# mLSTM row sums in a two-layer hybrid trunk: VectorE adds the overlapping blocks of the weights, TensorE multiplies their sum by ones

## The chip, the cores and the metric

The kernel runs on one core of a Trainium2 chip. The metric is the device time of one launch in microseconds (us), lower is better. Engines are named as in the profile: PE is TensorE (PEld its weight loads), DVE is VectorE, ACT is ScalarE, POOL is GpSimd, SP is SyncE, which here only starts loads of weights.

## The reference, cut to what matters

The program is a decoder trunk of two layers over 512 tokens and a width of 2048. Each layer projects the normalised input to 7944 columns, runs four groups of mixers on them (latent attention, RWKV-7, mLSTM, differential attention), gates them, and projects back. The change is in the mLSTM group, which has four heads of width 128. The reference works it in chunks of 64 tokens with a carried state. What it computes of one head is this:

```python
D = b[..., :, None] - b[..., None, :] + ig[..., None, :]
D = jnp.where(mask, D, -jnp.inf)
...
s = jnp.einsum('bhcjd,bhcsd->bhcjs', q, k) * jnp.exp(D - m_j[..., None])
num = jnp.einsum('bhcjs,bhcsv->bhcjv', s, v) + ...   # state carried from earlier chunks
den = jnp.sum(s, axis=-1) + ...
h = num / jnp.maximum(jnp.abs(den), jnp.exp(-m_j))[..., None]
```

`den` is the sum of the weights of each query token over all key tokens up to it. The kernel leaves the chunks away and forms the whole causal 512 x 512 matrix of weights of a head at once, with key tokens on the partitions, and then needs its sum over the keys, once for every query token, spread over all 128 partitions.

## The kernel before, in words

TensorE has one long job, and small ones are slipped into it. The long job is the projections: 640 steps of weights in two layers (one step is 128 rows of the contraction and up to 512 columns of weights), each with 4 tiles (one group has 3) of three 512-column matmuls (weights and activations are split in a high and a low half, `w_hi`, `w_lo`, `h_hi`, `h_lo`; L769, and L784 for the output projection). SyncE loads each step into `raw`. GpSimd makes both halves of it (L728 the high one, L738 the low one, which subtracts the high half from `raw`); there are four buffers of halves, so GpSimd runs at most four steps ahead of TensorE. ScalarE copies a finished group of projections out of PSUM (L1218) and stores it.

The small jobs are the mixers. Between two of their steps TensorE runs a number of projection tiles that is written down in a table (`FILL`), by `fill(name, head)`; these tiles are what it does while VectorE and ScalarE work on the mixer. Every engine runs its instructions in the written order and waits on semaphores; `link` makes VectorE wait for its own last instruction.

One head of the mLSTM goes like this, with its lines:

- L1120 and L1121: two matmuls spread the gates over the partitions. VectorE takes a running maximum (L1913, L1914), forms four blocks of exponents in `ml_w` (L1917) and finishes q and k (L1923). TensorE runs `fill("ml_qk")` meanwhile. ScalarE exponentiates `ml_w` (L1537, L1539).
- L1127: four matmuls give the scores. Key block i (128 keys on the partitions) meets only queries from i * 128 on, so the blocks are 512, 384, 256 and 128 columns wide. VectorE multiplies them by `ml_w` into `ml_s` (L1927) and masks the diagonal block (L1928), and the last of these raises `s_ml_s_ready`. TensorE runs `fill("ml_s")` meanwhile, 8, 7, 7 or 6 tiles.
- L1135: four matmuls, 1280 columns together, add values times weights into PSUM bank 0. L1138: four matmuls of the same widths multiply the weights by a matrix of ones into bank 1, which is the sum over the keys; the last raises `s_ml_num_mm`. All of them are plain fp32, which the trace shows as two matmul instructions each.
- VectorE meanwhile runs the convolution of the next head's q and k, eight instructions (L1901 and L1903), except in the last head. Then it waits for `s_ml_num_mm`, forms the denominator (L1936, L1937), its reciprocal (L1938), `ml_h` (L1939) and its square (L1940). TensorE runs `fill("ml_h")` meanwhile, 14, 13, 12 or 11 tiles.
- L1145: one matmul by ones sums the squares. ScalarE makes the norm's factor (L1263, L1264), then runs what the table gives it (`fill("ml_gate")`), and VectorE gates the head (L1943, L1944, L1624 to L1636). Then the next head begins with L1120, which waits for the gate's L1631.

In the first head the fill's last tiles finish a group of projections: ScalarE copies three of its four tiles out before the norm's factor and the fourth behind it, and TensorE's next group waits for these copies.

Of the kernel before, what the change touches and what calls it, by code (L numbers as in the profile page):

```python
# [27 lines left out]
P = 128  # L28
D, T, DEPTH = 2048, 512, 2
NT = T // P  # L30
# [287 lines left out]
def build(nc, a, out):  # L318

    with ExitStack() as ctx:  # L320
# [50 lines left out]
        ps = ctx.enter_context(nc.psum_tensor("ps", [P, 4, 512], F32))  # L371
# [6 lines left out]
        ident, ones, bones = const("ident"), const("ones"), const("bones")  # L378
# [119 lines left out]
        ml_ucol = rg(NT, 4)  # L498
        ml_m, ml_nf = rg(T), rg(T)
        ml_w = rg(NT, T)  # L500
        ml_s = rg(NT, T)
        ml_h, ml_den, ml_sq = rg(T), rg(T), rg(T)
        ml_o, ml_oe, ml_rs = rg(T), rg(T), rg(T)
# [129 lines left out]
        s_ml_s_ready = sem("ml_s_ready")  # L633
        s_ml_num_mm = sem("ml_num_mm")
# [42 lines left out]
        for layer in range(DEPTH + 1):  # L677
# [9 lines left out]
            with nc.Block() as block:  # L687
# [54 lines left out]
                def _(pe):  # L742
                    mm, turn = nc.tensor.matmul, nc.tensor.transpose
# [87 lines left out]
                    for k in range(4):  # L831
                        for i in range(NT):
                            if not tail and k == 0:
                                pe.wait_ge(s_x_loaded[i], 16)
                            last = turn(ps[:, k, i * P:(i + 1) * P], x_tok[:, i, k * P:(k + 1) * P], ident)
                        last.then_inc(s_x_turned, 1)
                    for n, tiles in enumerate(ROWS_OF_MEAN):
                        pe.wait_ge(s_rs_diag, n + 1)
                        mm(ps_proj[:, n, tiles.start * P:tiles.stop * P], ones, rs_diag[:, tiles, :],
                           start=True, stop=True).then_inc(s_rs_mm, 1)  # L840
                    pe.wait_ge(s_rs_ready, 2)
                    for k in range(4, KT):
                        pe.wait_ge(s_h_scaled, k - 3)
                        for i in range(NT):
                            last = turn(ps[:, k % 4, i * P:(i + 1) * P], x_tok[:, i, k * P:(k + 1) * P], ident)
# [12 lines left out]
                    for half in (slice(0, 64), slice(64, P)):  # L858
                        last = mm(ps[half, 2, :], rot_mla[half, :], la_peg[half, :], start=True, stop=True)
# [7 lines left out]
                    for i in range(NT):  # L867
                        for j in range(2):
                            last = mm(ps[:, i, :], la_in[:, 3 + j, i * P:(i + 1) * P],
                                      la_wkv[:, j, :].rearrange("p (h c) -> p h c", h=HEADS)[:, :, P:2 * P],  # L870
                                      start=(j == 0), stop=(j == 1))
# [17 lines left out]
                    for h in range(HEADS):  # L889
# [8 lines left out]
                        for j in range(2):  # L898
                            last = mm(ps[:, 2, :], la_wkv[:, j, h * 256:h * 256 + P], la_in[:, 3 + j, :],
                                      start=(j == 0), stop=(j == 1))  # L900
# [40 lines left out]
                    for hp in range(4):  # L941
# [53 lines left out]
                        for i in range(NT):  # L995
                            for q, o in swapped:
                                last = mm(ps[o, 3, i * 64:(i + 1) * 64], ident[q, q], rw_xt[q, 4 + i, :],
                                          start=True, stop=True)
# [118 lines left out]
                    for h in range(HEADS):  # L1117
                        if h:
                            pe.wait_ge(s_y_ready, 8 + h)
                        mm(ps[:, 0, :], sel_u[0:36, h * P:(h + 1) * P], ml_gt[0:36, :], start=True, stop=True)  # L1120
                        mm(ps[:, 1, :], sel_f[64:100, h * P:(h + 1) * P], ml_gt[64:100, :], start=True, stop=True  # L1121
                           ).then_inc(s_ml_u_mm, 1)
                        fill("ml_qk", h)
                        pe.wait_ge(s_ml_max, h + 1)
                        pe.wait_ge(s_ml_qk_ready, h + 1)
                        for i in range(NT):
                            last = mm(ps[:, i, i * P:T], ml_acc[:, 1, i * P:(i + 1) * P], ml_acc[:, 0, i * P:T],  # L1127
                                      start=True, stop=True)
                        last.then_inc(s_ml_scores_mm, 1)
                        fill("ml_s", h)  # L1130
                        pe.wait_ge(s_ml_s_ready, h + 1)
                        if h == 0:
                            pe.wait_ge(s_ml_first_loaded, 16)
                        for i in range(NT):
                            mm(ps[:, 0, i * P:T], ml_v[:, i, h * P:(h + 1) * P], ml_s[:, i, i * P:T],  # L1135
                               start=(i == 0), stop=(i == NT - 1))
                        for i in range(NT):
                            last = mm(ps[:, 1, i * P:T], ones, ml_s[:, i, i * P:T],  # L1138
                                      start=(i == 0), stop=(i == NT - 1))
                        last.then_inc(s_ml_num_mm, 1)  # L1140
                        if h == 0:
                            fill("to_z_ml")
                        fill("ml_h", h)
                        pe.wait_ge(s_ml_h_sq, h + 1)
                        mm(ps[:, 2, :], ones, ml_sq, start=True, stop=True).then_inc(s_ml_h_sum, 1)  # L1145
                        fill("ml_gate", h)
# [462 lines left out]
                def _(dve):  # L1609
# [3 lines left out]
                    def link(ins):  # L1613

                        counts[0] += 1
                        ins.then_inc(s_dve_order, 1)
                        dve.wait_ge(s_dve_order, counts[0])
# [292 lines left out]
                    for h in range(HEADS):  # L1910
# [15 lines left out]
                        for i in range(NT):  # L1926
                            link(v.scalar_tensor_tensor(out=ml_s[:, i, i * P:T], in0=ps[:, i, i * P:T], scalar=0.25 * float(P) ** -0.5, in1=ml_w[:, i, i * P:T], op0=MUL, op1=MUL))  # L1927
                            ins = v.tensor_tensor(ml_s[:, i, i * P:(i + 1) * P], ml_s[:, i, i * P:(i + 1) * P], causal, MUL)  # L1928
                            if i == NT - 1:
                                ins.then_inc(s_ml_s_ready, 1)  # L1930
                            else:
                                link(ins)
                        if h < HEADS - 1:
                            convolve(h + 1)
                        dve.wait_ge(s_ml_num_mm, h + 1)
# [91 lines left out]
```

## Time and profile before

| what | value |
|---|---|
| median of 3 runs | 2431.85 us (2427.43 to 2432.50) |
| the profiled execution | 2427.41 us, its span 2425.6 us |
| PE busy | 2351.5 us, 97% of the span |
| POOL, DVE, ACT busy | 1732.2, 1158.1, 634.4 us (71%, 48%, 26%) |
| mean granted clock of TensorE | 0.993 |
| DMA | 117 GB/s on average |

The profiled execution is at the lower end of the three timed ones. TensorE is the engine that is busy nearly all the time. The page's slices of TensorE's clock are all 9, that is 90% or more of full speed; the short spells at half speed are seen only in narrower windows. A line of the timeline says when a group of like instructions began, how long it took from the first begin to the last end, and in square brackets how long the engine had been idle before it and what released it. Matmuls overlap, so the pace is read from one begin to the next.

### The profile page before, as it was taken

The numbers are of one execution on the slowest core, as the hardware profiler recorded it, in microseconds if no ns is written. First come the engines' busy times: TensorE is split into PE (matmuls) and PEld (weight loads), VectorE is DVE, ScalarE is ACT, GpSimd is POOL, SyncE is SP. The second block draws the span as 40 slices with busy tenths as digits, with TensorE's granted clock in tenths as the row PEclk, the third lists the DMA queues.
The fourth block names the chain that finished last, engine by engine and source line by source line (L and its number), as shares of the span: only waits on it lengthen the run. The fifth ranks groups of instructions, "written<-read, shape, count | busy, mean of one in ns | idle before, by whom it ended". The sixth has DMA issues, their size and how long they took to land. (4 is left out here: it accounts for less than half of the span.)

```text
span 2425.6 us, 38853 instructions
## 1 busy us (share of the span) xinstructions
PE 2351.5 (97%) x16320; PEld 1770.0 (73%) x16320; DVE 1158.1 (48%) x1505; ACT 634.4 (26%) x1124; POOL 1732.2 (71%) x1228
## 2 busy tenths in 40 slices
PE   7999999999999999999999999999999999999999
PEld 5767677777777677777777677777777777777777
DVE  5123345557463675454250232466475547745442
ACT  4222222121221222333241223222122212324321
POOL 3676688668587778777637666877596787888774
PEclk9999999999999999999999999999999999999999
DMA  4623243233233435632445232533232243474223
GB/s 153 189 78 100 79 152 117 75 89 104 81 105 119 127 111 192 218 86 68 140 110 166 79 109 88 157 97 97 67 113 84 84 142 112 133 252 140 79 73 123
DMA packets 163568, 284.18 MB, mean 117 GB/s; under 512 B 28408, under 2 KB 35960, under 8 KB 161856
## 3 DMA queue, kind: packets, MB, share of 16 engines
q1 hardware_dynamic: 108352, 180.93, 26.6%
q10 hardware_dynamic: 55040, 100.77, 12.1%
q8 instruction: 128, 2.10, 0.4%
q14 instruction: 48, 0.39, 0.0%
HBM read 229.97 MB, written 51.64 MB: 116 GB/s over the span
## 5 line engine op out<-in xcount | busy, mean ns | idle before, releaser
L728 POOL TENSOR_SCALAR w_hi<-raw 128x512 fp32r<-128x512 f32 x552 | 903.7, 1637 | 490.8 <-PE ps_proj L769 404.7
L738 POOL TENSOR_TENSOR w_lo<-raw,w_hi 128x512 fp32r<-128x512 f32 (+1 forms) x640 | 832.8, 1302 | 155.0 <-ACT w_hi L1228 99.5
L769 PE MATMUL ps_proj<-h_hi,w_hi 128*128 128x512 f32 (+1 forms) x1760 | 734.8, 418 | 8.0 <-ACT stage L1218 5.0
L769 PE MATMUL ps_proj<-h_lo,w_hi 128*128 128x512 f32 (+1 forms) x1760 | 690.0, 392 | 0.0
L769 PE MATMUL ps_proj<-h_hi,w_lo 128*128 128x512 f32 x1728 | 676.9, 392 | 0.0
L769 PEld LDWEIGHTS ps_proj<-h_hi,w_hi 128*128 128x128 f32 (+1 forms) x1760 | 330.3, 188 | 112.4 <-issue 26.3
L769 PEld LDWEIGHTS ps_proj<-h_lo,w_hi 128*128 128x128 f32 (+1 forms) x1760 | 330.2, 188 | 74.1
L769 PEld LDWEIGHTS ps_proj<-h_hi,w_lo 128*128 128x128 f32 x1728 | 326.3, 189 | 68.7 <-issue 11.1
L784 PE MATMUL ps_proj<-w_hi,h_hi 128*128 128x512 f32 x448 | 184.6, 412 | 9.6 <-DVE arena L1644 9.2
L784 PE MATMUL ps_proj<-w_hi,h_lo 128*128 128x512 f32 x448 | 176.3, 393 | 0.0
L784 PE MATMUL ps_proj<-w_lo,h_hi 128*128 128x512 f32 x448 | 175.8, 392 | 0.0
L784 PEld LDWEIGHTS ps_proj<-w_hi,h_hi 128*128 128x128 f32 x448 | 85.0, 190 | 31.5 <-issue 14.1
L1218 ACT ACTIVATE stage<-ps_proj 128x512 f32<-128x512 f32 (+1 forms) x118 | 70.5, 597 | 136.2 <-PE ps_proj L769 113.8
L769 PE MATMUL ps_proj<-w_hi,h_hi 128*128 128x512 f32 x256 | 104.9, 410 | 0.0
L769 PE MATMUL ps_proj<-w_lo,h_hi 128*128 128x512 f32 x256 | 99.8, 390 | 0.0
L769 PE MATMUL ps_proj<-w_hi,h_lo 128*128 128x512 f32 x256 | 99.8, 390 | 0.0
L784 PEld LDWEIGHTS ps_proj<-w_lo,h_hi 128*128 128x128 f32 x448 | 85.0, 190 | 19.7 <-issue 3.4
L784 PEld LDWEIGHTS ps_proj<-w_hi,h_lo 128*128 128x128 f32 x448 | 84.8, 189 | 18.3
L1717 DVE TENSOR_REDUCE arena<-ps 128x1 f32<-128x128 f32 (+3 forms) x96 | 47.1, 490 | 85.6 <-PE ps L921 60.6
L1228 ACT ACTIVATE w_hi<-raw 128x512 fp32r<-128x512 f32 (+1 forms) x88 | 48.7, 561 | 148.1 <-PE ps_proj L769 75.5
L1263 ACT ACTIVATE arena<-ps 128x512 f32<-128x512 f32 x24 | 14.4, 598 | 242.7 <-PE ps L1102 129.0
L1591 ACT ACTIVATE arena<-ps,arena 128x128 f32<-128x128 f32 (+3 forms) x64 | 38.7, 615 | 129.5 <-DVE arena L1718 129.5
(347 smaller groups left out, 3160.0 us busy)
## 6 DMA issues: line engine op xcount, KB each, us to landing
raw<-in_w_in_dram SPq DMA_DIRECT2D x480, 256.0 KB, 2.7
raw<-in_w_out_dram SPq DMA_DIRECT2D x128, 256.0 KB, 3.0
projected<-stage ACTq DMA_DIRECT2D x116, 256.0 KB, 2.8
arena<-projected ACTq DMA_DIRECT2D x90, 256.0 KB, 3.1
out_dram<-arena ACTq DMA_DIRECT2D x7, 1024.0 KB, 4.8
gated_hi<-arena ACTq DMA_DIRECT2D x24, 256.0 KB, 2.7
gated_lo<-arena ACTq DMA_DIRECT2D x24, 256.0 KB, 3.2
h_hi<-gated_hi SPq DMA_DIRECT2D x8, 768.0 KB, 12.9
```

Of the source, the lines that this page charges most:

```text
L728: nc.gpsimd.tensor_scalar(hi, src, 1.0, None, ALU.mult).then_inc(s_hi_split, 1)
L738: nc.gpsimd.tensor_tensor(lo, src, hi.bitcast(F32), ALU.subtract).then_inc(s_raw_split, 1)
L769: last = mm(ps_proj[rows, m, :], lhsT, rhs, start=(k == 0 and j == 0), stop=(k == KT - 1 and j == len(products) - 1))
L784: last = mm(bank[:, i, :], lhsT, rhs, start=(first and j == 0), stop=(last_k and j == 2))
L1218: nc.scalar.activation(stage[0:rows, m, :], ps_proj[0:rows, m, :], ACT.Copy).then_inc(s_proj_copied, 1)
L1228: nc.scalar.activation(w_hi[:, at_all % N_SPLIT, 0:width], raw[:, at_all % N_RAW, 0:width], ACT.Copy).then_inc(s_hi_by_act, 1)
L1263: link(nc.scalar.activation(dst, src, ACT.Ln, scale=1.0 / n, bias=eps))
L1591: nc.scalar.activation(da_p[:, b, 0:(i + 1) * P], ps[:, b, 0:(i + 1) * P], ACT.Exp, scale=da_rq[:, 4 * half + b:4 * half + b + 1], bias=da ...
L1717: link(v.tensor_reduce(mx[:, b:b + 1], ps[:, b, 0:(i + 1) * P], AX, MAX))
```

## The change

VectorE adds the four blocks of `ml_s` where they overlap. For queries 0 to 127 only block 0 has weights; for queries from 128 on the first addition takes blocks 0 and 1 (384 columns), the second adds block 2 (256), the third block 3 (128). The sum lies in row 0 of `ml_w`, which is free by then. TensorE multiplies 128 columns of block 0 and 384 columns of the sum by ones, in place of 1280 columns. The semaphore `s_ml_s_ready` is raised twice in a head, after the masked weights and after the sum. Everything else, the table of fills too, stays as it is.

```diff
         ml_w = rg(NT, T)
+        ml_sum = ml_w[:, 0, :]
...
                         fill("ml_s", h)
-                        pe.wait_ge(s_ml_s_ready, h + 1)
+                        pe.wait_ge(s_ml_s_ready, 2 * h + 1)
...
-                        for i in range(NT):
-                            last = mm(ps[:, 1, i * P:T], ones, ml_s[:, i, i * P:T],
-                                      start=(i == 0), stop=(i == NT - 1))
-                        last.then_inc(s_ml_num_mm, 1)
+                        mm(ps[:, 1, 0:P], ones, ml_s[:, 0, 0:P], start=True, stop=True)
+                        pe.wait_ge(s_ml_s_ready, 2 * h + 2)
+                        mm(ps[:, 1, P:T], ones, ml_sum[:, P:T], start=True, stop=True).then_inc(s_ml_num_mm, 1)
...
+                        dve.wait_ge(s_ml_s_ready, 2 * h + 1)
+                        link(v.tensor_tensor(ml_sum[:, P:T], ml_s[:, 0, P:T], ml_s[:, 1, P:T], ADD))
+                        link(v.tensor_tensor(ml_sum[:, 2 * P:T], ml_sum[:, 2 * P:T], ml_s[:, 2, 2 * P:T], ADD))
+                        v.tensor_tensor(ml_sum[:, 3 * P:T], ml_sum[:, 3 * P:T], ml_s[:, 3, 3 * P:T], ADD).then_inc(s_ml_s_ready, 1)
                         if h < HEADS - 1:
                             convolve(h + 1)
```

TensorE's instructions around the first head's products, before (L769 is a projection tile, `ps<-arena` the values, `ps<-arena,always` the ones):

```order
L769 MATMUL ps_proj<-h_lo,w_hi 128x512
L1135 MATMUL ps<-arena 128x512 [waits ml_first_loaded,ml_s_ready]
L1135 MATMUL ps<-arena 128x384
L1135 MATMUL ps<-arena 128x256
L1135 MATMUL ps<-arena 128x128
L1138 MATMUL ps<-arena,always 128x512
L1138 MATMUL ps<-arena,always 128x384
L1138 MATMUL ps<-arena,always 128x256
L1138 MATMUL ps<-arena,always 128x128
L769 MATMUL ps_proj<-h_hi,w_hi 128x512
```

And with the change, where all lines of this part are one further down:

```order
L770 MATMUL ps_proj<-h_lo,w_hi 128x512
L1136 MATMUL ps<-arena 128x512 [waits ml_first_loaded,ml_s_ready]
L1136 MATMUL ps<-arena 128x384
L1136 MATMUL ps<-arena 128x256
L1136 MATMUL ps<-arena 128x128
L1138 MATMUL ps<-arena,always 128x128
L1140 MATMUL ps<-arena,always 128x384 [waits ml_s_ready]
L770 MATMUL ps_proj<-h_hi,w_hi 128x512
```

Four matmuls by ones have become two, and the second of them has a wait of its own.

VectorE's instructions in the same place, from the last weights to the denominator, before (L1901 and L1903 are the next head's convolution, L1936 reads the products):

```order
L1927 SCALAR_TENSOR_TENSOR arena<-ps,arena 128x128 [waits dve_order]
L1928 TENSOR_TENSOR arena<-arena 128x128 [waits dve_order]
L1901 TENSOR_SCALAR arena<-arena,par 128x512 [waits ml_qk_loaded]
L1903 SCALAR_TENSOR_TENSOR arena<-arena,par 128x512 [waits dve_order] x3
L1901 TENSOR_SCALAR arena<-arena,par 128x512 [waits dve_order]
L1903 SCALAR_TENSOR_TENSOR arena<-arena,par 128x512 [waits dve_order] x3
L1936 SCALAR_TENSOR_TENSOR arena<-ps,arena 128x512 [waits ml_num_mm]
```

And with the change (L1934 to L1936 are the additions, L1940 is what was L1936):

```order
L1927 SCALAR_TENSOR_TENSOR arena<-ps,arena 128x128 [waits dve_order]
L1928 TENSOR_TENSOR arena<-arena 128x128 [waits dve_order]
L1934 TENSOR_TENSOR arena<-arena 128x384 [waits ml_s_ready]
L1935 TENSOR_TENSOR arena<-arena 128x256 [waits dve_order]
L1936 TENSOR_TENSOR arena<-arena 128x128 [waits dve_order]
L1901 TENSOR_SCALAR arena<-arena,par 128x512 [waits ml_qk_loaded]
L1903 SCALAR_TENSOR_TENSOR arena<-arena,par 128x512 [waits dve_order] x3
L1901 TENSOR_SCALAR arena<-arena,par 128x512 [waits dve_order]
L1903 SCALAR_TENSOR_TENSOR arena<-arena,par 128x512 [waits dve_order] x3
L1940 SCALAR_TENSOR_TENSOR arena<-ps,arena 128x512 [waits ml_num_mm]
```

The three additions stand ahead of the convolution, and so ahead of all that VectorE does for the denominator and the squares.

## Rows read from the trace of the kernel before

**Rows 1.** The page's first part: busy time, share and count.
```profile
PE 2351.5 (97%) x16320; PEld 1770.0 (73%) x16320; DVE 1158.1 (48%) x1505; ACT 634.4 (26%) x1124; POOL 1732.2 (71%) x1228
```

**Rows 2.** TensorE's waits: for whom, us in total, times, longest.
```profile
PE ps L1127 <- DVE arena L1923: 6.4, 4, 2.8
...
PE ps L1145 <- DVE arena L1940: 1.2, 4, 0.3
```

**Rows 3.** Timeline, TensorE, first head: start, duration, count, idle before.
```profile
808.46 2.32 PE L1135 MATMUL ps<-arena 128*128 128x512 f32 x8
810.61 2.32 PE L1138 MATMUL ps<-arena,always 128*128 128x512 f32 x8
...
822.36 1.02 PE L1145 MATMUL ps<-arena,always 128*128 128x512 f32 x2
```

**Rows 4.** Timeline, VectorE, first head.
```profile
806.50 0.29 DVE L1928 TENSOR_TENSOR arena<-arena 128x128 f32<-128x128 f32 x1
...
814.44 0.68 DVE L1936 SCALAR_TENSOR_TENSOR arena<-ps,arena 128x512 f32<-128x512 f32 x1
...
820.00 1.44 DVE L1940 TENSOR_TENSOR arena<-arena 128x512 f32<-128x512 f32 x1
```

**Rows 5.** Timeline, ScalarE, first head.
```profile
823.30 0.60 ACT L1218 ACTIVATE stage<-ps_proj 128x512 f32<-128x512 f32 x1 [0.46 <-ACT stage L1218]
...
825.58 0.60 ACT L1263 ACTIVATE arena<-ps 128x512 f32<-128x512 f32 x1
...
828.03 0.58 ACT L1218 ACTIVATE stage<-ps_proj 128x512 f32<-128x512 f32 x1
```

**Rows 6.** VectorE's groups by shape: busy us, mean ns, idle before.
```profile
L1927 DVE SCALAR_TENSOR_TENSOR arena<-ps,arena 128x384 f32<-128x384 f32 x8 | 4.5, 558 | 0.3
L1927 DVE SCALAR_TENSOR_TENSOR arena<-ps,arena 128x256 f32<-128x256 f32 x8 | 3.4, 425 | 0.3
```

**Rows 7.** Timeline, second head, around the matmul of the squares.
```profile
862.74 1.29 POOL L738 TENSOR_TENSOR w_lo<-raw,w_hi 128x512 fp32r<-128x512 f32 x1
863.12 1.46 DVE L1940 TENSOR_TENSOR arena<-arena 128x512 f32<-128x512 f32 x1
...
864.63 1.12 PE L1145 MATMUL ps<-arena,always 128*128 128x512 f32 x2 [0.34 <-DVE arena L1940]
```

**Rows 8.** Timeline, third head.
```profile
890.11 1.62 DVE L1901 TENSOR_SCALAR arena<-arena,par 128x512 f32<-128x512 f32 x1
890.18 1.26 POOL L738 TENSOR_TENSOR w_lo<-raw,w_hi 128x512 fp32r<-128x512 f32 x1
...
896.38 2.02 POOL L728 TENSOR_SCALAR w_hi<-raw 128x512 fp32r<-128x512 f32 x1 [4.93 <-PE ps_proj L769]
...
903.27 1.13 PE L1145 MATMUL ps<-arena,always 128*128 128x512 f32 x2 [0.25 <-DVE arena L1940]
```

**Rows 9.** Timeline, VectorE, fourth head.
```profile
931.33 0.69 DVE L1936 SCALAR_TENSOR_TENSOR arena<-ps,arena 128x512 f32<-128x512 f32 x1 [4.68 <-PE ps L1138]
```

**Rows 10.** Timeline, TensorE: idle spells and what follows them.
```profile
371.04 0.66 PE L945 MATMUL ps<-arena 32*128 32x512 f32 x1 [3.19 <-ACT arena L1432]
...
828.66 0.50 PE L769 MATMUL ps_proj<-h_hi,w_hi 128*128 128x512 f32 x1 [2.52 <-ACT stage L1218]
...
835.95 0.69 PE L1120 MATMUL ps<-arena 36*128 36x512 f32 x1
...
2029.20 0.50 PE L769 MATMUL ps_proj<-h_hi,w_hi 128*128 128x512 f32 x1 [2.52 <-ACT stage L1218]
...
2034.89 0.69 PE L1120 MATMUL ps<-arena 36*128 36x512 f32 x1
...
2377.73 0.47 PE L784 MATMUL ps<-w_hi,h_hi 128*128 128x512 f32 x1 [2.18 <-PEq L2002]
```

**Rows 11.** Windows of 2 us: busy PE, PEld, DVE, ACT, POOL; PEclk, DMA, GB/s.
```profile
830.00:832.00 2.00, 2.00 (x6) 1.52 (x6) 1.93 (x3) 0.00 (x0) 1.92 (x2) 0.50 0.08 31
...
2030.00:2032.00 2.00, 2.00 (x10) 1.65 (x9) 1.92 (x3) 0.00 (x0) 1.67 (x1) 1.00 0.35 131
```

## The prediction

> **What bounds the kernel now.** The page's first part comes first: TensorE is busy for 2351.5 us of a span of 2425.6, 97%, and VectorE for about half of it [rows 1]. So an instruction taken from TensorE is a gain unless TensorE then waits for somebody else, and the next view is the list of its waits. Two of its lines lie in the mLSTM: TensorE waits for VectorE four times, 1.2 us in all, ahead of L1145, the sum of the squares, and at L1127 [rows 2]. L1145 stands right behind the place of the change, and what it waits for is VectorE's chain, which the change makes longer. So the third view is the timeline of each head, TensorE beside VectorE, to find how much room is left at L1145. Both layers show the same four heads within 0.1 us, apart from spells of slow clock, so I work out one layer and double it.
>
> **What TensorE saves.** L1135 begins at 808.46 and L1138 at 810.61: 2.15 us for 1280 columns of fp32 [rows 3]. The matmuls by ones fall from 1280 to 512 columns, so 768/1280 x 2.15 = 1.29 us a head go, 10.3 us over eight heads.
>
> **What VectorE gets.** Three additions of 384, 256 and 128 columns. The nearest rows are L1927 with two inputs and the same widths, 558 and 425 ns [rows 6], and L1928, which is just such an addition of two blocks in SBUF: 0.29 us for 128 columns [rows 4]. With some 0.04 us between linked instructions: 0.56 + 0.43 + 0.29 + 0.12 = 1.40 us a head. That is the low end. The high end is from L1940: 1.44 and 1.46 us in the first two heads [rows 4, 7], where L1936 with as many columns takes 0.68 [rows 4]. It overlaps a subtraction of GpSimd's: it runs from 862.74 to 864.03 and L1940, begun at 863.12, ends at 864.58, half a microsecond behind it [rows 7]. L1901 at 890.11 takes 1.62 us and ends 0.3 us behind the subtraction of 890.18 to 891.44 [rows 8]. Less 0.56 us or so for its own work, that is a hold of about 1.1 us, and the one of L1940 is 0.8. One such meeting more or less is the unknown in each head: 1.4 us, or 2.5.
>
> The Trainium skill, on the page "SBUF — State Buffer", section "Who interferes with whom", gives the rule behind this: a VectorE instruction with two SBUF inputs contends with a GpSimd instruction that reads SBUF, and the later one waits for the whole of the earlier. The rows above agree in the length of the hold. All three additions are of that kind, and the multiplications with a PSUM input, whose durations stand in for them in the low sum, are not; by the rule alone the low end is too low whenever a subtraction is under way.
>
> **The new wait on the sum** (the 384-column matmul) costs nothing while TensorE is still busy ahead of it with L1135 and 128 columns of ones, 2.15 + 0.21 = 2.4 us against 1.4 to 2.5 us of additions. I take nothing; the end is 0.2 us a head, and it would be hidden by the next wait in three heads.
>
> **Head by head.** What counts is when L1145 can begin, the later of TensorE's own arrival and the end of L1940.
>
> First head. L1940 ends at 820.00 + 1.44 = 821.44 and L1145 begins at 822.36 [rows 3, 4], so there is room of 0.9 us. With the change L1940 ends at 822.8 to 823.6, since the convolution is what L1936 follows at 814.44 (the products are done near 810.61 + 2.15 = 812.8), and TensorE is there at 821.1: a new idle spell of about 2 us. It isn't lost, though. Behind L1145 TensorE stands still again, for 2.52 us until 828.66, for a copy by ScalarE [rows 10], and ScalarE's order is: three copies paced by projection tiles (the third at 823.30), L1263 at 825.58, the fourth copy at 828.03 [rows 5]. Those tiles come 1.29 us earlier, L1263 could begin at 824.3, and L1145's 1.02 us are over by 823.9 to 824.7. So the restart at 828.66 moves up by 0.9 to 1.3 us. I take -1.1.
>
> Second head. TensorE already waits 0.34 us at L1145 [rows 7], so every microsecond on VectorE is one on the path, and TensorE's 1.29 us turn into idle. VectorE is late by 1.4 us. L1940 then begins near 864.5. Whether it is held there as it is now (it is at 863.12) depends on GpSimd, whose work moves 1.3 us ahead with TensorE's and whose next subtraction then begins at about the same moment: +0.7 if it isn't held, +1.7 if it is. I take +1.2.
>
> Third head. Again L1145 waits, 0.25 us, and L1940 isn't held now. GpSimd's high half at 896.38 waits for TensorE [rows 8] and moves to 895.1, so its subtraction comes near 897, where VectorE, 1.4 us late, is now still in the convolution: one hold of about 1 us more. +1.4 to +2.5; I take +2.2.
>
> Fourth head. No convolution; L1936 waits 4.68 us for the products [rows 9], so the additions are covered and everything moves up: -1.3.
>
> Sum of a layer: -1.1 + 1.2 + 2.2 - 1.3 = +1.0 us, of two +2.0. With all low ends it is -1.3 + 0.7 + 1.4 - 1.3 = -0.5, with all high ones -0.9 + 1.7 + 2.5 - 1.3 = +2.0; times two, -1.0 to +4.0.
>
> **TensorE's clock.** After some idle spells TensorE runs at its lower level, 1.2 GHz: PEclk is 0.50 at 830 us, behind the 2.52 us of idle before 828.66, and 1.00 at 2030 us behind the same spell in the other layer [rows 10, 11]. From the restart to the next head's L1120 it is 7.29 us with the slow clock and 5.69 without, so one such spell costs 1.6 us [rows 10]. Past the start of the program there are nine idle spells of over 2 us, the first 3.19 us long and the last 2.18 [rows 10], and five of them are followed by it. The change makes new ones: about 2 us in the first head, 0.34 + 1.29 + 1.2 = 2.8 us in the second, 0.25 + 1.29 + 2.2 = 3.7 us in the third. What the first costs goes into ScalarE's wait; what the second costs goes mostly into the third's own wait, and TensorE's wait at 828.66, now with 1.6 us of slow clock behind it, shrinks to under 1 us, which saves about 1 us. The third has nothing behind it that takes it up. At two chances in three it is 2 x 2/3 x 1.6 = 2.1 us. Together +1.1 us, from -1.6 to +3.2.
>
> **The forecast** is +2.0 + 1.1 = +3.1 us: the profiled execution of 2427.41 us would become 2430.5. It is the lowest of what is shown, 4.4 us below the median of 2431.85, so in terms of the median it is 2435.0 us. TensorE's 10.3 us are then spent: half of them as idle time in the second and third heads, and the rest given back by the same heads' longer chain.
>
> **Rivals.**
> The whole saving arrives: L1145's waits don't grow, because the additions fit in room I have missed. 2431.85 - 10.3 = 2421.6 us. For it: the share of busy time, 97% against 48% [rows 1]. Against it: L1145 already waits in two heads of each layer [rows 2], and in these the additions are ahead of it in VectorE's order. Chance 0.08.
>
> Slower: the holds by GpSimd and the slow clock both come. One more hold in each of the second and third heads makes +4.0, a slow spell behind the third in both layers +3.2, and behind the second partly (another 1 us each) +2: 9.2 us, 2441.0 us. It decides from about 5 us on, that is from one slow spell and the high ends together. For it: the idle of 3.7 us would be longer than any that the trace shows past the start. Against it: GpSimd runs earlier too and the holds may miss. Chance 0.34.
>
> A new wait at the 384-column matmul takes over: the additions meet a subtraction in every head and end behind L1135. That is 0.5 us in the fourth head and in the first, where nothing follows it up, 2 us in all beside the forecast, 2437 us. Against it: 2.4 us of cover. Chance 0.04. The forecast itself has 0.54, with 2431 to 2439 as its own range.
>
> **How the numbers follow.** A change of 0.2%, 4.9 us, is about what a measurement of this kernel can tell from none. Of the forecast's 0.54 some 0.09 lie above that and nothing below; of the slower rival's 0.34 some 0.27 lie above. So slower 0.37, faster 0.10 (the first rival and a little of the forecast's scatter), same 0.53. The range reaches from 2428.5, some way towards the whole saving, to 2442.
>
> **What would show it.** Right: TensorE's mean saving in L1138 and its successor (0.86 us of columns in place of 2.15); waits at L1145 of 2 to 4 us in the second and third heads of both layers, about 2 us in the first, none in the fourth; the wait for ScalarE's copy below 1 us. Wrong: no wait at L1145 above 1 us (then the saving arrives), or waits at the 384-column matmul. The clock's share is seen as windows with PEclk 0.50 behind the third head's wait. If both layers show no slow clock there the time is nearer 2432; if VectorE's convolution isn't lengthened by holds, nearer 2431.

## The result and the profile after

The changed kernel takes 2442.83 us, the median of 7 runs (2437.68 to 2446.35); the kernel before has 2430.57 us in 7 runs (2427.39 to 2434.45). The ratio is 1.0045, with a 95% interval of 1.0031 to 1.0059 (it is worked out from all executions and not from the medians alone, here and below): slower, by 12.3 us in the medians and by 11.0 us in the means (2441.64 against 2430.62). The forecast was 2435.0 us, +3.1, with a range up to 2442, at whose upper end the result lies. The direction was right; the size is nearest to that of the second rival (2441.0).

TensorE has 32 matmuls fewer. These are the parts of the page and of TensorE's waits that answer to [rows 1, 2]:

```profile
PE 2354.1 (96%) x16288; PEld 1770.3 (73%) x16288; DVE 1172.0 (48%) x1529; ACT 634.3 (26%) x1124; POOL 1731.4 (71%) x1228
```
```profile
PE ps L1145 <- DVE arena L1944: 16.5, 6, 4.2
...
PE ps L1128 <- DVE arena L1923: 5.5, 2, 2.7
...
PE ps_proj L770 <- ACT stage L1218: 1.8, 2, 0.9
```

The wait for VectorE ahead of the squares (L1145) has grown from 1.2 us to 16.5 us in six waits; the wait for ScalarE's copy has shrunk from 2.52 us to 0.92 us at the longest ([rows 10]). TensorE is busy for 2.6 us longer in spite of 32 matmuls less: a busy microsecond counts the same at the slow clock.

TensorE's timeline in the first layer, to be read beside [rows 3, 7, 8] (L1136 is the products with the values, L1138 and L1140 the two by ones; L1145 appears once for each head):

```profile
811.45 2.32 PE L1136 MATMUL ps<-arena 128*128 128x512 f32 x8
813.60 0.39 PE L1138 MATMUL ps<-arena,always 128*128 128x128 f32 x2
813.82 0.81 PE L1140 MATMUL ps<-arena,always 128*128 128x384 f32 x2
825.54 1.12 PE L1145 MATMUL ps<-arena,always 128*128 128x512 f32 x2 [1.36 <-DVE arena L1944]
...
830.32 0.50 PE L770 MATMUL ps_proj<-h_hi,w_hi 128*128 128x512 f32 x1 [0.92 <-ACT stage L1218]
...
865.77 1.16 PE L1145 MATMUL ps<-arena,always 128*128 128x512 f32 x2 [2.71 <-DVE arena L1944]
...
908.43 2.08 PE L1145 MATMUL ps<-arena,always 128*128 128x512 f32 x2 [4.16 <-DVE arena L1944]
...
945.43 1.02 PE L1145 MATMUL ps<-arena,always 128*128 128x512 f32 x2
```

No line shows idle time ahead of L1140, so the new wait on the sum costs nothing. In the third head this is close: the last addition ends at 895.09 and L1140 begins at 895.18. In the third head L1145 takes 2.08 us where it takes 1.13 in [rows 8]: it runs at half clock. Windows of the stretches behind the second and third heads' waits show how long that lasts (columns as in [rows 11]):

```profile
866.00:868.00 2.00, 2.00 (x5) 1.23 (x5) 0.00 (x0) 1.02 (x2) 0.83 (x1) 0.68 0.10 10
868.00:870.00 2.00, 2.00 (x6) 1.61 (x5) 0.40 (x1) 1.49 (x2) 0.00 (x0) 0.50 0.40 121
```
```profile
908.00:910.00 2.00, 1.57 (x3) 0.84 (x3) 0.38 (x1) 0.00 (x0) 0.00 (x0) 0.50 0.30 107
910.00:912.00 2.00, 2.00 (x5) 1.34 (x4) 0.00 (x0) 1.44 (x2) 0.00 (x0) 0.50 0.00 0
912.00:914.00 2.00, 2.00 (x6) 1.62 (x5) 0.81 (x1) 1.07 (x2) 0.77 (x1) 0.50 0.00 0
```

The second layer has the same waits (1.35, 2.72 and 4.16 us) and two slow spells, from 2078 and from 2119.

VectorE's and GpSimd's timelines in the second head show the hold on the additions:

```profile
850.05 0.56 DVE L1934 TENSOR_TENSOR arena<-arena 128x384 f32<-128x384 f32 x1
850.64 1.38 DVE L1935 TENSOR_TENSOR arena<-arena 128x256 f32<-128x256 f32 x1
852.06 0.58 DVE L1936 TENSOR_TENSOR arena<-arena 128x128 f32<-128x128 f32 x1
```
```profile
850.18 1.56 POOL L739 TENSOR_TENSOR w_lo<-raw,w_hi 128x512 fp32r<-128x512 f32 x1
851.72 1.85 POOL L729 TENSOR_SCALAR w_hi<-raw 128x512 fp32r<-128x512 f32 x1
```

The second addition ends 0.28 us behind the subtraction that it met. The hold isn't all new: in the kernel before, the same subtraction met the convolution that stood in this place, whose three instructions took 3.45 us there and 2.33 us where nothing held them:

```profile
850.43 3.45 DVE L1903 SCALAR_TENSOR_TENSOR arena<-arena,par 128x512 f32<-128x512 f32 x3
```

The third addition overlaps GpSimd's next instruction, L729. It takes 0.58 us, where it takes 0.29 us in the third head with nothing beside it, and L729 takes 1.85 us in place of 1.49.

In the third head another subtraction falls into the second half of the convolution:

```profile
898.71 3.50 DVE L1903 SCALAR_TENSOR_TENSOR arena<-arena,par 128x512 f32<-128x512 f32 x3
```
```profile
899.35 1.29 POOL L739 TENSOR_TENSOR w_lo<-raw,w_hi 128x512 fp32r<-128x512 f32 x1
```

### The profile page after: what moved, and what is told of

Its sections match the earlier page's. It is cut to its first block and busy times, and to the rows that moved or that the text cites. A ratio compares the mean times of both kernels' runs of the same rounds, so it can differ in the third digit from the quotient of the medians.

```text
span 2441.0 us, 38813 instructions
## 1 busy us (share of the span) xinstructions
PE 2354.1 (96%) x16288; PEld 1770.3 (73%) x16288; DVE 1172.0 (48%) x1529; ACT 634.3 (26%) x1124; POOL 1731.4 (71%) x1228
## 5 line engine op out<-in xcount | busy, mean ns | idle before, releaser
L729 POOL TENSOR_SCALAR w_hi<-raw 128x512 fp32r<-128x512 f32 x552 | 898.0, 1627 | 503.9 <-PE ps_proj L770 420.7
L739 POOL TENSOR_TENSOR w_lo<-raw,w_hi 128x512 fp32r<-128x512 f32 (+1 forms) x640 | 837.6, 1309 | 158.0 <-ACT w_hi L1228 102.6
```

The source lines that it names most:

```text
L729: nc.gpsimd.tensor_scalar(hi, src, 1.0, None, ALU.mult).then_inc(s_hi_split, 1)
L739: nc.gpsimd.tensor_tensor(lo, src, hi.bitcast(F32), ALU.subtract).then_inc(s_raw_split, 1)
```

## Three measures for the comparison

One is the length from a head's products with the values to its squares, where VectorE's chain decides. The other is the length of the whole mLSTM section, from the first head's products to the fourth head's squares, in each layer, and what the slow clock takes in it (over the windows of 2 us, the sum of 2 x (1 - PEclk); a part of it falls into idle time and costs nothing). All are worked out from the timelines' begins and the windows of the profiled executions, in us:

| kernel | heads 1 to 4 | section, layer 1 and 2 | lost to slow clock in them |
|---|---|---|---|
| before | 13.90, 13.72, 13.02, 11.81 | 130.17, 128.62 | 1.7, 0 |
| the change | 14.09, 14.77, 15.73, 10.56 | 133.98, 133.33 | 5.1, 3.4 |
| additions alone | 14.11, 14.80, 14.63, 11.87 | 132.94, 132.90 | 1.7, 1.7 |
| TensorE's part alone | 12.56, 12.98, 13.25, 10.56 | 126.80, 125.49 | 1.7, 0 |
| change, TensorE kept busy | 14.09, 14.77, 15.73, 10.55 | 129.75, 130.23 | 0, 0 |
| change, convolution split | 12.58, 12.41, 11.95, 10.65 | 124.57, 126.07 | 0, 1.7 |
| before, convolution split | 13.90, 13.22, 12.60, 11.92 | 130.52, 130.52 | 1.7, 1.7 |

The heads are those of the first layer. The second layer's agree within 0.13 us, but for the kernel kept busy, whose first and third heads are 13.59 and 14.77 there.

The third, from which the cost of one slow spell is read best, is the length from one head's products to the next head's, in us:

| kernel | second to third, layer 1 and 2 | third to fourth, layer 1 and 2 |
|---|---|---|
| before | 39.34, 39.34 | 36.57, 36.58 |
| the change | 41.70, 41.72 | 42.17, 41.43 |
| change, second head alone kept busy | 40.37, 40.39 | 41.30, 40.87 |
| change, third head alone kept busy | 41.69, 40.38 | 39.29, 39.27 |

The 40.38 holds an unfilled wait of 2.72 us that no slow spell followed, and the kernel with all heads kept busy has 39.28 in its first layer. So 40.38 and 39.28 are the lengths of the change's own chain, +1.04 and +2.7 us, and what lies above them is slow clock.

## The experiments

Theory A: VectorE's chain ends in the matmul of the squares; what it gets longer lands there in the second and third heads, and TensorE's saved time becomes idle time that is followed by slow clock. Theory B: the loss comes from somewhere else, such as the split matmuls, or it is the clock's scatter. A and B are told apart by doing one part alone, and by keeping TensorE busy without touching VectorE's chain. Each kernel was timed beside the kernel before, in five rounds.

### The additions alone

```diff
-                        mm(ps[:, 1, 0:P], ones, ml_s[:, 0, 0:P], start=True, stop=True)
-                        pe.wait_ge(s_ml_s_ready, 2 * h + 2)
-                        mm(ps[:, 1, P:T], ones, ml_sum[:, P:T], start=True, stop=True).then_inc(s_ml_num_mm, 1)
+                        for i in range(NT):
+                            last = mm(ps[:, 1, i * P:T], ones, ml_s[:, i, i * P:T],
+                                      start=(i == 0), stop=(i == NT - 1))
+                        last.then_inc(s_ml_num_mm, 1)
```

> VectorE makes its three additions a head, but TensorE still multiplies all four blocks by ones (1280 columns) and the sum is not used. Theory A (the matmul of the squares waits at the end of VectorE's chain, and what VectorE gets longer lands there): in each layer nothing in the first head (its restart hangs on ScalarE's copies), +1.0 to +1.2 us in the second, +2.0 to +2.7 in the third, nothing in the fourth: +7 us for two layers, and +2 to +4 for spells of slow clock behind the new idle times, so about 2440 us (+9, 0.4%). Theory B (the additions are hidden, and the loss of the change comes from elsewhere, such as the split matmuls or the clock's own scatter): 2430 us, within 2 us of the kernel before.

Measured: 2437.13 us against 2430.88, ratio 1.0025 (1.0015 to 1.0034). TensorE's waits at the squares (L1146 here):

```profile
867.92 1.12 PE L1146 MATMUL ps<-arena,always 128*128 128x512 f32 x2 [1.43 <-DVE arena L1945]
...
908.16 1.12 PE L1146 MATMUL ps<-arena,always 128*128 128x512 f32 x2 [1.87 <-DVE arena L1945]
```

The second head is 1.08 us longer, the third 1.61, the fourth 0.06, so each layer is some 2.7 us longer: A is right in place and B is out. The expected 9 us are 6. The third head got only 1.6 us: without TensorE's saving GpSimd doesn't run ahead, and its subtraction meets only the end of the longer convolution (three instructions in 2.56 us, not 3.50). And no slow spell followed the waits of 1.4 to 1.9 us at the squares, in either layer.

### TensorE's part alone

```diff
-                        for i in range(NT):
-                            last = mm(ps[:, 1, i * P:T], ones, ml_s[:, i, i * P:T],
-                                      start=(i == 0), stop=(i == NT - 1))
-                        last.then_inc(s_ml_num_mm, 1)
+                        mm(ps[:, 1, 0:P], ones, ml_s[:, 0, 0:P], start=True, stop=True)
+                        mm(ps[:, 1, P:T], ones, ml_s[:, 0, P:T], start=True, stop=True).then_inc(s_ml_num_mm, 1)
```

> No additions; TensorE multiplies by ones 512 columns of block 0 alone, so the sum over the other key blocks is left out. Theory A: TensorE's 1.29 us a head arrive in the first head (by way of ScalarE's copies) and in the fourth, and become idle time in the second and third, where VectorE's chain sets the matmul of the squares: 4 x 1.29 = 5.2 us, 2425.5 us, with waits of about 1.6 us at that matmul in the second and third heads. Theory B (TensorE is the bound everywhere): 8 x 1.29 = 10.3 us, 2420 us.

Measured: 2426.49 us against 2430.88, ratio 0.9983 (0.9974 to 0.9993). The first and fourth heads are 1.3 us shorter, the second 0.7, and the third is 0.2 us longer. The timeline shows who waits:

```profile
863.38 1.13 PE L1143 MATMUL ps<-arena,always 128*128 128x512 f32 x2 [0.94 <-DVE arena L1938]
...
902.25 1.12 PE L1143 MATMUL ps<-arena,always 128*128 128x512 f32 x2 [1.75 <-DVE arena L1938]
```

Less than half of the 10.3 us arrives even with nothing added. In the third head GpSimd comes 1.3 us earlier and meets the end of the convolution:

```profile
893.48 2.56 DVE L1901 SCALAR_TENSOR_TENSOR arena<-arena,par 128x512 f32<-128x512 f32 x3
```
```profile
895.66 1.52 POOL L738 TENSOR_TENSOR w_lo<-raw,w_hi 128x512 fp32r<-128x512 f32 x1
```

That costs 0.2 us. Each part alone makes the subtraction graze the convolution; only both together, GpSimd earlier and VectorE later, put it in the middle. This meeting, 3.50 us against 2.56, is most of the 1.1 us by which the change's third head (15.73) is longer than that of the additions alone (14.63). It is read from the timelines; no run took the subtraction away.

### TensorE kept busy ahead of the squares

```diff
+                        for _ in range((1, 3, 4, 0)[h]):
+                            mm(ps[:, 3, :], ones, ml_v[:, 0, :], start=True, stop=True)
                         pe.wait_ge(s_ml_h_sq, h + 1)
```

> The change, with matmuls of no use (ones by values, 512 columns of fp32, 0.86 us each, into a PSUM bank that nobody reads then) ahead of the wait for the squares: 1, 3, 4 and 0 of them in the four heads, to fill idle times of 1.36, 2.71 and 4.16 us. Theory A with the clock as its second part: the waits of VectorE stay, so the moves of +1.2 us a layer stay, but no slow clock follows in the mLSTM's second and third heads: 1.2 + 2.9 us less in the first layer, about the same in the second, so about 2436 us, 6 to 7 below the change. If the slow clock is no consequence of these idle times, or costs nothing there, it stays at 2443 us; if the filled matmuls delay the squares it is above that.

Measured: 2430.99 us against 2430.88, ratio 1.0002 (0.9993 to 1.0010): 11.8 us less than the change in the medians. In the third head, the squares are L1147 here:

```profile
906.46 1.13 PE L1147 MATMUL ps<-arena,always 128*128 128x512 f32 x2 [0.75 <-DVE arena L1946]
```
```profile
906.00:908.00 2.00, 1.54 (x5) 0.97 (x6) 0.41 (x1) 0.38 (x1) 0.00 (x0) 1.00 0.34 112
908.00:910.00 2.00, 2.00 (x11) 1.62 (x10) 0.00 (x0) 1.97 (x3) 0.86 (x1) 1.00 0.00 0
```

Adding matmuls that compute nothing makes the kernel faster. In the first layer the chain is as long as in the change (15.73 us in the third head), the granted clock stays at 1.00, which is 2.4 GHz, and the section is 4.2 us shorter. So the chain alone costs 1.1 us over a section without slow clock (128.62), and the rest is slow clock. In the second layer the section is 3.1 us shorter and the comparison less clean: GpSimd's subtraction held VectorE ahead of the third head's products (TensorE waits 2.11 us there) and not behind them, which is why that head is 14.77 and the section 0.5 us longer than the first layer's. The sections give 7.3 of the 11.8 us. The gain is larger than the 6 to 7 us that were expected, and where the rest of it lies isn't shown.

### One head at a time kept busy

The same edit with (0, 3, 0, 0) and with (0, 0, 4, 0) matmuls.

> The change, with three matmuls of no use in the second head alone, ahead of the wait of 2.71 us. In the change's trace that wait is followed by about 1.2 us of loss by slow clock, and my step said it would be taken up by the third head's wait, which the trace denies: so 1.2 us a layer less, 2440.5 us; by my step as predicted, 2443. If keeping busy helps only where the idle time is above 4 us, also 2443.

> The change, with four matmuls of no use in the third head alone, ahead of the wait of 4.16 us. If the long slow spell behind it (2.9 us of loss in the first layer, one of 1.2 to 1.7 in the second) is the larger part of what the change costs, 4 to 6 us less: 2437 to 2439 us. If both heads count alike, 2439 to 2440.

Measured against 2430.06 us: 2437.63 for the second head (1.0036, 1.0023 to 1.0049), 2434.61 for the third (1.0025, 1.0016 to 1.0035): 5.2 and 8.2 us less than the change, both more than expected. Their sections are 131.89 and 131.34 us, and 131.05 and 129.74. The second of these kernels has no slow spell at all in its second layer, though its second head's wait of 2.72 us is unfilled there, so its sections don't price the third head's spell alone; the lengths from products to products do. The spell behind the second head's wait costs 1.3 us each time (41.7 against 40.38). The one behind the third's costs 2.9 and 2.2 us in the change (42.17 and 41.43 against 39.28), and 2.0 and 1.6 us with the second head kept busy. Both were there in both layers of the change. My step that the second's would vanish in the third's own wait is wrong.

### The convolution split

```diff
-                            convolve(h + 1)
+                            convolve(h + 1, (0,))
...
                         v.tensor_tensor(ml_sq, ml_h, ml_h, MUL).then_inc(s_ml_h_sq, 1)
+                        if h < HEADS - 1:
+                            convolve(h + 1, (1,))
```

`convolve` with (0,) makes q's half, with (1,) k's. First on top of the change, then on the kernel before.

> The change, and of the next head's convolution only q's half stands behind the additions; k's half (four instructions, 2.9 us) stands behind the squares, where VectorE waits 3.9 to 6.8 us for ScalarE anyway. Theory A: the chain to the squares is 2.9 to 4 us shorter than in the change, so the waits of 1.4 and 2.7 us at their matmul are gone and that of 4.2 us nearly; all of TensorE's 10.3 us arrive, and 1 to 2 us of old waits with them: 2418 to 2421 us. If k's half only moves the delay to the gate behind it (VectorE's idle time there is too short, or GpSimd holds it), the wait comes back at the scores of the next head: 2427 us or more.

> The kernel before (no additions, 1280 columns by ones) with the convolution split as in the kernel with the change and a split convolution. There the matmul of the squares waits only 0.34 and 0.25 us, so by theory A little is to be had: 1 to 2 us less than before, 2429 to 2430. The distance to the change with the split convolution (6.2 us below the kernel before) is then what the change brings once its chain has room: about 5 us, up to 10.3 if nothing is lost. If the split does all of the 6.2 us by itself, this one is at 2425.

Measured: on the change 2424.70 us against 2430.88 (0.9975, 0.9965 to 0.9986), 18 us under the change itself and 4 to 7 us above what was expected. On the kernel before 2434.04 us against 2430.06 (1.0019, 1.0010 to 1.0027). The table of lengths says what happened. With the split, the second and third heads of the change are 12.41 and 11.95 us, and the squares wait 0.36 and 0.39 us. In the kernel before there was little to be had at the squares, and what the split gave there came back at the scores, to where k's half is now pushed: the waits ahead of them are

```profile
PE ps L1127 <- DVE arena L1924: 7.7, 6, 2.7
```

against [rows 2]. The change with the split pays there too (7.3 us at these scores, 5.5 in the change). So the change is a gain of about 9 us (2434.04 to 2424.70, medians of two sets of runs) once VectorE's chain has room for it, and the split a gain only together with it. Why the split alone should cost 4 us isn't shown: its sections are 2.3 us longer in all, of which a slow spell is 1.7.

### One tile more ahead of the squares

```diff
-    ... ml_h=(14, 13, 12, 11), ml_gate=(12, 12, 12, 12),
+    ... ml_h=(15, 13, 12, 11), ml_gate=(11, 12, 12, 12),
```

On top of the change with the split.

> The change with the split convolution, and in the first head one projection tile more ahead of the squares (15 and 11 in place of 14 and 12). ScalarE then copies the fourth tile of the group ahead of the norm's factor, and the wait of 2.52 us behind it should go, in both layers, with its slow spells: 5 us less, 2419 to 2421 us. If ScalarE's chain to the gate gets so much longer by the copy (1.05 us) that the second head's L1120 waits for it, half of that is given back.

Measured: 2430.03 us against 2430.06 (0.9999, 0.9986 to 1.0011), where 2419 to 2421 were expected, and 5.3 us more than with 14 tiles (in another set of runs). The wait for the copy is gone, and it is back at the next head's begin, with longer slow clock behind it:

```profile
831.30 0.94 PE L1121 MATMUL ps<-arena 36*128 36x512 f32 x1 [2.68 <-DVE arena L1631]
```
```profile
832.00:834.00 2.00, 2.00 (x6) 0.83 (x3) 1.29 (x2) 0.00 (x0) 0.00 (x0) 0.50 0.88 319
834.00:836.00 2.00, 2.00 (x6) 1.55 (x5) 1.90 (x4) 1.44 (x2) 1.15 (x1) 0.50 0.96 287
836.00:838.00 2.00, 2.00 (x6) 1.52 (x6) 1.93 (x3) 0.77 (x2) 1.62 (x2) 0.50 0.68 255
```

The first head is a chain of ScalarE and VectorE longer than TensorE's work beside it; moving a tile moved the wait.

### Matmuls of no use in the other idle spells

Ahead of the first head's scores, where TensorE waits 2.75 us in all these kernels, and in one kernel ahead of the wait of 2.68 us above as well (the same loop for h == 1 ahead of L1121's wait):

```diff
+                        for _ in range(0 if h else 3):
+                            mm(ps[:, 3, :], sel_u[0:36, 0:P], ml_gt[0:36, :], start=True, stop=True)
                         pe.wait_ge(s_ml_max, h + 1)
```

> The change with the split convolution, and in the first head three matmuls of no use (36 rows, 512 columns of fp32, 0.86 us each) ahead of the scores, where TensorE stands idle for 2.77 us in every kernel of this study, before too. A spell of slow clock followed in the first layer (PEclk 0.50 at 800 us) and none in the second. If such spells cost 1.6 us each and come behind one idle spell in two, 1.5 to 3 us less than the same kernel without them: 2422 to 2423 us. If only idle spells of over 4 us matter, 2424.7.

> The change with the split convolution and 15 tiles ahead of the first head's squares, whose wait of 2.5 us had only moved (from ScalarE's copy to L1121 at the second head's begin, 2.7 us) and was followed by long slow spells (4 us at PEclk 0.50 from 832, 3 us from 2036). Three matmuls of no use ahead of each layer's scores in the first head and three ahead of L1121 in the second. If the 5.3 us by which this placing was slower than 14 tiles are the clock's, they are gone, 2422 to 2424 us; if they are the copy's longer chain, it stays at 2430.

> The kernel before with the same three matmuls of no use ahead of the first head's scores, nothing else. It tells what the slow clock behind an idle spell that the change doesn't touch costs: 1.5 to 3 us less than before, 2427.5 to 2429, if that is 1.6 us a spell; 2430.5 if it is nothing.

Measured: the split change 2422.43 us against 2429.87 (0.9961, 0.9949 to 0.9973); with 15 tiles 2422.80 (0.9965, 0.9953 to 0.9977), 7.2 us less than without the filling; the kernel before 2430.22 (0.9998, 0.9988 to 1.0009), no gain where 1 to 3 us were expected. The split change without the filling had 0.9975 (0.9965 to 0.9986), so its own gain isn't clear of the noise. The kernel with 15 tiles is the one that gained: its slow clock behind L1121 went from 3.4 to 1.7 us a layer, by the windows, and what the other half of its 7.2 us is isn't shown. The idle time ahead of the scores went in all three, but in the first layer the slow spell there didn't; in the second it was there in the split change alone. A window of the split change with the filling, first layer:

```profile
802.00:804.00 2.00, 2.00 (x4) 0.87 (x3) 0.00 (x0) 0.84 (x3) 0.41 (x1) 0.50 0.68 172
```

The last kernel takes other matmuls for the same place: `range(0 if h else 4)` of `mm(ps[:, 3, 0:ALWAYS], ones, always[:], ...)`.

> As the kernel with three matmuls of 36 rows ahead of the first head's scores, but with four of 128 rows and 386 columns (0.65 us each, 2.6 us together). There the idle time was gone and PEclk fell to 0.50 near 802 and 2000 us all the same. If it matters to the clock that the matmuls of no use have 36 rows (in the third head, where those with 128 rows filled 4.2 us, no slow spell followed), there is none here: no window with PEclk 0.50 between 795 and 810 us nor in the second layer's place, and 2419 to 2421 us. If filling this place doesn't help, whatever is put there: slow spells again, 2422 to 2424 us.

Measured: 2422.37 us against 2431.80 (0.9963, 0.9951 to 0.9976), the best median, and not to be told from 2422.43. The spell is gone there, in both layers:

```profile
800.00:802.00 2.00, 1.84 (x7) 0.84 (x5) 1.76 (x3) 1.27 (x3) 1.92 (x2) 1.00 0.75 236
802.00:804.00 2.00, 2.00 (x7) 1.20 (x8) 0.00 (x0) 0.91 (x3) 0.93 (x1) 1.00 0.68 153
```

Another spell stands behind the wait of 2.5 us for ScalarE's copy, which no matmul fills: PEclk 0.50 from 830 and from 2028 us. The split change with the 36 rows has none there, in either layer. So the number of spells in the profiled executions is the same, and the time too. One execution each can't tell whether the one spell replaced the other or came by chance.

## Why the prediction was right in direction and short in size

**What bounds it.** Right: the wait at L1145 is the step that decided, in the second and third heads, in both layers.

**TensorE's saving.** 1.29 us a head predicted. L1138 and L1140 take 0.39 and 0.81 us in the timeline, where [rows 3] has 2.32, and the fourth head, which shows it undisturbed, is 1.25 us shorter (11.81 to 10.56).

**The additions** take 0.56 + 1.38 + 0.58 us in the second head, the upper end of the 1.4 to 2.5 predicted, and 2.54 and 2.35 us in the first and third. Their unheld lengths are 0.56, 0.43 and 0.29 us, just those of the rows that stood in for them (L1928 was a multiplication by the mask and no addition, with the same length). But the subtraction that now holds them had held the convolution before, so most of this hold was no new cost. The rule of the Trainium skill ("SBUF — State Buffer", "Who interferes with whom") agrees with the trace for GpSimd's subtraction: the second addition ends 0.28 us behind it. It doesn't for L729, which reads SBUF too: the third addition begins 0.34 us behind the begin of L729 and ends 0.93 us ahead of its end, and is only 0.29 us longer than alone.

**The heads.** First head: the restart behind the copy is 18.87 us after the products (811.45 to 830.32) in place of 20.20, so -1.33, predicted -1.1; the wait at L1145 is 1.36 us in place of the 2 us foreseen. Second: 14.77 against 13.72, +1.05, predicted +1.2. This one is luck in part: the +1.2 was the middle between a square that is held (+1.7) and one that isn't (+0.7). It isn't held (L1944 takes 0.69 us, L1940 took 1.46), and VectorE reaches it 1.8 us late, not 1.4. Third: 15.73 against 13.02, +2.7, predicted +2.2, with a range to +2.5. Fourth: -1.25, predicted -1.3. The sum is +1.2 a layer, predicted +1.0, and the sections without slow clock have +1.1 (129.75 in the first layer of the kernel kept busy, 129.74 in the second of the one with the third head kept busy, against 128.62). The mechanism in the third head was the one predicted: GpSimd runs ahead with TensorE, and its subtraction of 899.35 to 900.64 holds the convolution.

**The clock** is the term that was mis-sized: +1.1 us for both layers was forecast. The sections lost 8.5 us to slow clock in place of 1.7 in the profiled executions, and by the kernel kept busy they would be 7.3 us shorter without it. From products to products the four spells cost 1.3 + 1.3 + 2.9 + 2.2 = 7.7 us; less the spell of 1.6 us behind the first head's copy, which is gone as foreseen, that is +6.1 us, and with the chain's 2.4 us it makes the 8.5 by which the sections are longer. Two things were wrong in the step. The spell behind the second head's wait isn't absorbed: TensorE reaches the next head's first matmuls late, and VectorE's work for that head waits for them:

```profile
877.77 1.22 DVE L1913 TENSOR_TENSOR_SCAN arena<-always,ps 128x512 f32<-128x512 f32 x1 [2.44 <-PE ps L1122]
```

And the one behind the third head's wait came in both layers and cost 2.9 and 2.2 us, where I had 1.6 us and two chances in three. The 2.9 is a single spell of over 6 us, from 908 to 914. The wait of 4.2 us isn't shown to be the reason for its length: three others like it were followed by spells of the usual length, and in the kernel before, one of 2.63 us at 2335.55 was followed by a long one.

**The sum.** The sections are 3.81 + 4.71 = 8.5 us longer. The medians are 12.3 apart, the two profiled executions 15.4 (spans 2441.0 and 2425.6), so 6.9 us of these lie outside the sections: 3.0 ahead of the first layer's, 7.0 between them, and 3.1 less behind the second layer's. The slow clock by the windows outside the sections is 15.4 us in both, but 3.4 us of that of the kernel before is at the program's start, where the change's windows show none although its tiles run at half pace until 30 us. Beyond the start it is 15.4 against 12.0. The spells are behind waits that both kernels have: those of 1.97 and 2.62 us near 1094 and 1143 us are followed by one in the change and not in the kernel before, and their like in the second layer the other way round. Whether that is caused by the change or is one execution's luck isn't settled: beyond the start it was 9 to 17 us in the experiments, in no order that I can explain.

**The rivals.** The whole saving didn't arrive, by the waits foreseen. The slower rival was right in its second half (slow clock behind both waits) and wrong in its first: it had +2.0 us a layer by one more hold in each of the two heads, and the chain has +1.2. The new wait at the 384-column matmul didn't come.

## What to carry to other kernels

Before work is moved from the busiest engine to a half-idle one, find the next place where the busiest waits for it, and the room there. Here it was none in two heads of four, and both the moved work and the time saved went there. Behind the waits of 2.72 and 4.16 us here TensorE paid a second time, in slow clock, and that was two to three times the chain's own cost (3.1 us a layer more than before, against 1.2). Give the chain room first (here, four instructions moved into VectorE's idle time), and the change that cost 12 us is a gain: 0.25% in all under the kernel before, 0.4% with the idle spell ahead of the scores filled, a difference that isn't clear of the noise.

## What the runs showed of the hardware

- Matmuls that compute nothing, put into TensorE's idle time, took 11.8 us off a kernel of 2443 us.
- What they are may matter. With 36 rows they filled the 2.7 us ahead of the first layer's scores and PEclk still fell to 0.50 there, in the traces of three kernels; with 128 rows it stayed at 1.00, in both layers of one kernel. It is one profile of each, and of the ten kernels without filling there one has no spell in the first layer, and six have none in the second.
- A wait of the same length is not always followed by slow clock. The one of 2.72 us in the second head was in three of four cases, the one of 4.16 us in the third head in four of four, those of 1.4 to 1.9 us at the squares in none.
- A slow spell took 1.7 us by the windows in most cases and 3.4 us in some, behind idle times of 4.16 and 2.68 us, and of 2.63 us in the kernel before.
- GpSimd's subtraction (L739) holds a VectorE instruction with SBUF inputs until 0.28 to 0.55 us behind its own end (L1935 and, in the kernel before, L1940). GpSimd's high half (L729) doesn't hold it to its end: beside L1936 (0.58 us, alone 0.29) it grew from 1.49 to 1.85 us itself.
